# Gate tiles between the heads of the latent attention, and its values as hi/lo halves in f32r

## The reference, cut to what matters

```
proj = rmsnorm(x, ln_g) @ w_in
c_q, c_kv, k_rope, gate = split(proj, [384, 640, 672])
q  = rmsnorm(c_q) @ w_q_up
kv = rmsnorm(c_kv) @ w_kv_up            # k_nope and v per head
q, k = rope(rmsnorm(q)), rope(rmsnorm(concat(k_nope, k_rope)))
o  = causal_softmax_attention(q, k, v)
x  = x + (o * silu(gate)) @ w_out
```

## Time and profile before

| | us |
|---|---|
| median of 3 runs | 1353.39 (1350.48 to 1353.78) |
| the profiled execution, its own time | 1351.43 |
| its span from first to last instruction | 1349.6 |
| TensorE busy | 1317.7 (98%) |
| VectorE busy | 751.0 (56%) |
| ScalarE busy | 622.7 (46%) |
| GpSimd busy | 282.0 (21%) |

### The profile page before, as it was taken

How to read it: one execution, slowest core, us unless ns; L and a number is a source line. 1 busy time by engine, 2 the same in 40 slices (tenths; PEclk the granted TensorE clock), 3 DMA queues, 4 the chain that set the end, 5 groups by cost and what they waited for, 6 DMA issues and landing times. The chain is left out here.

```text
span 1349.6 us, 18281 instructions
## 1 busy us (share of the span) xinstructions
PE 1317.7 (98%) x6494; PEld 1095.5 (81%) x6494; DVE 751.0 (56%) x1236; ACT 622.7 (46%) x1108; POOL 282.0 (21%) x343
## 2 busy tenths in 40 slices
PE   7999999999999999999999999999999999999997
PEld 6989777788888888888888878888888888878876
DVE  5445688833753235798444643336467237578734
ACT  5336866622532234898244423424334224346534
POOL 2101844100000006674000000000000000677510
PEclk9999999999999999999999999999999999999999
DMA  5423200022222232001222323331333322311111
GB/s 189 115 67 106 70 1 0 1 94 94 94 94 94 94 98 88 18 0 32 103 101 93 95 78 98 105 94 51 95 108 103 110 94 63 110 43 37 35 60 63
DMA packets 63515, 104.05 MB, mean 77 GB/s; under 512 B 3428, under 2 KB 21080, under 8 KB 63320
## 3 DMA queue, kind: packets, MB, share of 16 engines
q1 hardware_dynamic: 62384, 99.44, 23.2%
q0 software_dynamic: 944, 3.65, 0.9%
q10 hardware_dynamic: 120, 0.05, 0.0%
HBM read 101.03 MB, written 2.10 MB: 76 GB/s over the span
## 5 line engine op out<-in xcount | busy, mean ns | idle before, releaser
L1531 DVE TENSOR_TENSOR w_lo<-stage,w_hi 128x1024 fp32r<-128x1024 f32 (+4 forms) x188 | 223.7, 1190 | 450.7 <-ACT w_hi L1016 450.7
L1016 ACT ACTIVATE w_hi<-stage 128x1024 fp32r<-128x1024 f32 (+4 forms) x188 | 191.8, 1020 | 475.4 <-PE ps L469 475.0
L467 PE MATMUL ps<-a0h,w_hi 128*128 128x512 f32 x448 | 177.4, 396 | 3.0 <-DVE q_lo L2061 3.0
L468 PE MATMUL ps<-a0l,w_hi 128*128 128x512 f32 x448 | 174.8, 390 | 0.0
L469 PE MATMUL ps<-a0h,w_lo 128*128 128x512 f32 x448 | 174.8, 390 | 0.0
L2133 POOL TENSOR_TENSOR small<-small 128x16 f32<-128x16 f32 (+2 forms) x15 | 33.4, 2224 | 504.2 <-DVE small L1609 360.0
L467 PEld LDWEIGHTS ps<-a0h,w_hi 128*128 128x128 f32 x448 | 84.4, 188 | 22.1 <-issue 4.7
L467 PE MATMUL ps<-w_hi,a0h 128*128 128x512 f32 x256 | 101.2, 395 | 0.0
L467 PE MATMUL ps<-a1h,w_hi 128*128 128x512 f32 x256 | 99.9, 390 | 0.3 <-DVE w_lo L1531 0.3
L469 PE MATMUL ps<-w_hi,a0l 128*128 128x512 f32 x256 | 99.7, 389 | 0.0
L468 PE MATMUL ps<-w_lo,a0h 128*128 128x512 f32 x256 | 99.6, 389 | 0.0
(11 more groups left out here) (313 smaller groups left out, 2980.4 us busy)
## 6 DMA issues: line engine op xcount, KB each, us to landing
stage<-in_a_w_in SPq DMA_DIRECT2D x48, 512.0 KB, 3.7
stage<-in_ple_w_gate SPq DMA_DIRECT2D x16, 512.0 KB, 3.3
stage<-in_w_kv_shared SPq DMA_DIRECT2D x16, 512.0 KB, 3.5
stage<-in_sb_w_in SPq DMA_DIRECT2D x16, 512.0 KB, 3.5
stage<-in_a_w_out SPq DMA_DIRECT2D x16, 512.0 KB, 3.3
stage<-in_b_w_in SPq DMA_DIRECT2D x16, 512.0 KB, 3.9
stage<-in_mla_w_in SPq DMA_DIRECT2D x8, 512.0 KB, 3.7
stage<-in_mla_w_out SPq DMA_DIRECT2D x8, 512.0 KB, 3.3
```

The lines of the kernel that those rows point to most:

```text
L467: pe.matmul(bank, wh, mh, start=start, stop=False)
L468: pe.matmul(bank, wh, ml, start=False, stop=False)
L1016: act.activation(slab(w_hi[r % 2], L, nk, w), slab(stage[r % 4], L, nk, w), ACT.Copy).then_inc(S("hi_ready"), 1)
L1531: dve.tensor_tensor(slab(w_lo[r % 2], L, nk, w), slab(stage[r % 4], L, nk, w), slab(w_hi[r % 2], L, nk, w), ALU.subtract)\
```

## The change

- `mla_gate` is cut in two. `mla_gate0` (tile 0) stands between `mla_cq` and `q_up`, `mla_gate1` (tiles 1 to 7) is made between the heads, two times two steps of k per head, in bank 7. The gate's loads are by tile: 128 columns of all eight row blocks.
- The transpositions of `proj` stand in `mla_cq` (8) and inside tile 0 (12). The squares are taken between the latents.
- The transposed probabilities are split: ScalarE rounds all 1280 columns to `prT_h`, VectorE subtracts to `prT_l`. The values of a head are 64 columns; `v_hl` holds their rounded half beside their rest as one operand of 128 columns (`mla_v` on ScalarE, `v_low` on GpSimd). A product therefore gives two halves of rows which have to be added: ScalarE copies one (`mla_part`), VectorE adds the other (`mla_sum`).
- Gate: VectorE scales a tile by half of the norm, ScalarE takes Tanh, GpSimd makes silu of it (`mla_silu`) and multiplies the head's output (`mla_gated`).
- One reciprocal for all four sums of a head; the scaled blocks follow after the last exponential.
- The transpositions of q and k go to bank 6, which the values use as well; q, k and values therefore wait for each other's readers.
- All steps of the heads are written out on every engine, without loops.
- The operand h of the layer stays in `a0h`, `a0l` (`H0 = A0`), and `pe_out0` moves.

The core of the diff:

```
@@ -192,12 +191,14 @@
     o_mh, o_ml = o_m[:, :, 0:T], o_m[:, :, T:2 * T]
     proj = put("proj", [P, MB, 672], 20)
     pr = put("pr", [P, TRI], 0)
-    prT = put("prT", [P, TRI], 5)
-    lat_sq = put("lat_sq", [P, MB, 672], 4)
+    prT_h, prT_l = put("prT_h", [P, TRI], 5, F32R), put("prT_l", [P, TRI], 4, F32R, of=SGM)
+    lat_sq = put("lat_sq", [P, MB, 672], 56)
     sq_tok = put("sq_tok", [P, MB, 4 * QK], 4, of=SGM)
     qT = [put(f"qT{s}", [P, T], 10 + 2 * s) for s in range(2)]
     kT = [put(f"kT{s}", [P, T], 14 + 2 * s) for s in range(2)]
-    v_pair = put("v_pair", [P, MB, P], 18)
+    q_tok_r = put("q_tok_r", [P, MB, HEADS * QK], 20, F32R)
+    v_hl = [put("v_hl0", [P, MB, P], 18, F32R), q_tok_r[:, :, 0:P]]
+    o_part = q_tok[:, :, 2 * QK:2 * QK + P]
     q_ring = [put(f"q_ring{s}", [P, MB, QK], 76 + 1.5 * s) for s in range(2)]
     k_ring = [put(f"k_ring{s}", [P, MB, QK], 79 + 1.5 * s) for s in range(2)]
     rope = put("rope", [P, 5, MB, ROPE], 82)
...
@@ -344,9 +345,10 @@
     LINEARS = [
         Linear("proj0", ins["ple_w_proj"][0], 2, columns(0, D), False, PT0, items("p0")),
         Linear("mla_cq", w_in, 8, columns(0, 672, 336), True, H0, items("h_mla")),
-        Linear("mla_gate", w_in, 8, columns(672, 1696), False, H0, items("h_mla")),
+        Linear("mla_gate0", w_in, 8, columns(672, 800), False, H0, items("h_mla"), by_tile=True),
         Linear("q_up", ins["mla_w_q_up"][0], 3, columns(0, HEADS * QK, 4 * QK), True, CQ[:3], IQ),
         Linear("kv_up", ins["mla_w_kv_up"][0], 2, columns(0, 2048), True, CQ[3:], IL),
+        Linear("mla_gate1", w_in, 8, [(800, 896)], False, H0, items("h_mla"), by_tile=True),
         Linear("out0", ins["mla_w_out"][0], 8, columns(0, D), False, OM, items("o_mla")),
         Linear("gate0", ins["ple_w_gate"][0], 8, columns(0, D), False, A1, items("x0")),
         Linear("sh_k", w_sh, 8, columns(0, D), False, A0, items("h_kv")),
...
+        def mla_gate_tile(L, j, bank, a, b):
+
+            r = L.load0 + j
+            if a == 0:
+                pe.wait_ge(S("lo_ready"), r + 1)
+                if j:
+                    pe.wait_ge(S("mla_gate1_read"), j)
+            wh, wl = slab(w_hi[r % 2], L, KD, P), slab(w_lo[r % 2], L, KD, P)
+            for k in range(a, b):
+                mm = three(ps[bank][:, :], wh[:, k, :], wl[:, k, :], *L.acts[k], k == 0, k == KD - 1)
+            if b == KD:
+                mm.then_inc(S("ring_used"), 1)
+
+        linear("mla_cq", 0, second={4: latents(0, 2)})
+        mla_gate_tile(lin["mla_gate0"], 0, 3, 0, 5)
+        latents(2, 5)()
+        mla_gate_tile(lin["mla_gate0"], 0, 3, 5, KD)
         linear("q_up")
...
+        def mla_values(h, first):
+            pe.wait_ge(S("pT_a"), 3 * h + 3)
+            pe.wait_ge(S("pT_b"), 3 * h + 3)
+            pe.wait_ge(S("v_ok"), h + 1)
+            pe.wait_ge(S("v_lo"), h + 1)
+            pe.wait_ge(S("kT_ok"), min(h + 3, HEADS))
             if not first:
                 pe.wait_ge(S("o_read"), h)
             for j in range(MB):
+                at = slice(KEY_COL[j], KEY_COL[j] + T - j * P)
+                pe.matmul(ps[6][:, j * P:T], v_hl[h % 2][:, j, :], prT_h[:, at], start=j == 0, stop=False, skip_group_check=True)
+                t = pe.matmul(ps[6][:, j * P:T], v_hl[h % 2][:, j, :], prT_l[:, at], start=False, stop=j == MB - 1, skip_group_check=True)
             t.then_inc(S("o_done"), 1)
 
+        def mla_step(h, s, i):
+
+            first, last = h == 0, h == HEADS - 1
+            mla_scores(h, s, first)
             if first:
                 pe.wait_ge(S(group_read[G + 3][0]), group_read[G + 3][1])
+            if not last:
+                mla_q(h + 1, 1 - s)
+            if i < PAIRS - 1:
+                mla_gate_tile(lin["mla_gate1"], i, 7, 4 * s, 4 * s + 2)
+            if not last:
+                mla_k(h + 1, 1 - s)
+            if i < PAIRS - 1:
+                mla_gate_tile(lin["mla_gate1"], i, 7, 4 * s + 2, 4 * s + 4)
             if not first:
+                mla_values(h - 1, h == 1)
+            mla_probs_T(h, first)
 
 
...
+        split_to(lin["q_up"].load0)
+        act.wait_ge(S("mla_cq_read"), 8)
+        latent_squares((0, 1))
+        latents(2, 4)
+        latent_squares((2, 3))
+        latents(4, 5)
+        split_to(lin["q_up"].load0 + 1)
+        act.wait_ge(S("mla_gate0_read"), 1)
+        act.activation(sgm[0][:, :], sgm[0][:, :], ACT.Silu).then_inc(S("sg_ready"), 1)
         act.wait_ge(S("lat_ok"), 1)
...
+            for b, (c, n) in enumerate(((0, T), (T, 384), (896, 384))):
+                act.activation(prT_h[:, c:c + n], ps[3 + b][:, 0:n], ACT.Copy).then_inc(S("pT_a"), 1)
...
+        def mla_step(h):
+            i, s = h // 2, h % 2
+            more = h < HEADS - 1
+            if h:
+                probs_T(h - 1)
+            probs(h, s, h == 0, (lambda: head_T(h + 1, 1 - s, "qT_done", qT, "q", "qT_ok")) if more else None)
+            if more:
+                head_T(h + 1, 1 - s, "kT_done", kT, "k", "kT_ok")
+            if h == 0:
                 k_squares(lin["kv_up"].n - 1)
-            if not first:
-                o_hi(i - 1, o_mh, "o_read", "o_mla")
-            probs(b, 1, between=None if last else lambda: head_T(a + 2, 0, "qT_done", qT, "q", "qT_ok"))
-            if not last:
-                head_T(a + 2, 0, "kT_done", kT, "k", "kT_ok")
-            probs_T(b)
-
-        mla_pair(0, first=True)
-        with act.Fori(1, PAIRS - 1) as i:
-            mla_pair(i)
-        mla_pair(PAIRS - 1, last=True)
+                mla_v(0)
+            if s == 0 and i < PAIRS - 1:
+                split_to(lin["mla_gate1"].load0 + i + 1)
+            if s == 0 and i:
+                mla_tanh(i)
+            if s and i:
+                o_hi(i - 1, o_mh, "o_gated", "o_mla")
+            if h:
+                mla_part(h - 1)
+            if more:
+                mla_v(h + 1)
...
+            dve.wait_ge(S("exp_done"), MB * h + MB)
+            link(dve.reciprocal(rsum, ssum))
+            for j in reversed(range(MB)):
                 at = slice(QRY_COL[j], QRY_COL[j] + (j + 1) * P)
                 dve.tensor_scalar(pr[:, at], pr[:, at], rsum[:, j:j + 1], None, ALU.mult).then_inc(S("p_ready"), 1)
...
-            dve.tensor_copy(prT[:, T:T + 384], ps[4][:, 0:384])
-            dve.tensor_copy(prT[:, T + 384:TRI], ps[5][:, 0:384]).then_inc(S("pT_b"), 1)
+            for b, (c, n) in enumerate(((0, T), (T, 384), (896, 384))):
+                dve.wait_ge(S("pT_a"), 3 * h + (b + 1))
+                dve.tensor_tensor(prT_l[:, c:c + n], ps[3 + b][:, 0:n], prT_h[:, c:c + n], ALU.subtract).then_inc(S("pT_b"), 1)
...
+        def mla_step(h):
+            i, s = h // 2, h % 2
+            maxima(h)
+            if h:
+                probs_T(h - 1)
+            normalize(h)
+            if h == 0:
                 head_sums(k_ss, 4 * HD, "k")(lin["kv_up"], G, MB - 1, None)
-            if not first:
+            if s == 0 and i < PAIRS - 1:
+                split_to(lin["mla_gate1"].load0 + i + 1)
+            if s and i < PAIRS - 1:
+                mla_gate_read(i + 1)
+            if s and i:
                 o_lo(i - 1, o_mh, o_ml, "o_mla")
-            normalize(b)
-            o_gate(a, 0, i, ps[6], "o_done", "o_read", "o_mla")
-            probs_T(b)
-
-        dve.wait_ge(S("sg_ready"), 8)
-        mla_pair(0, first=True)
-        with dve.Fori(1, PAIRS - 1) as i:
-            link.begin(i, 1, 16)
-            mla_pair(i)
-        link.end(PAIRS - 2)
-        mla_pair(PAIRS - 1)
+            if h:
+                mla_sum(h - 1)
...
+        for h in range(1, HEADS + 2):
+            if h > 1:
+                mla_gated(h - 2)
+            if h < HEADS:
+                v_low(h)
+            if h % 2 == 0 and 0 < h < HEADS:
+                mla_silu(h // 2)
+            if h + 3 < HEADS:
+                mla_head(h + 3, (h + 3) % 2, (h + 3) // 2)
+                pool.wait_ge(S("qk_ring"), 2 * h + 8)
 
...
```

More of the change, by code:

```diff
@@ L522, in group @@
                         pe.wait_ge(S("x_new"), 4 + n + 1)
+                    if L.name == "q_up" and g == k == 0 and n == 3:
+                        pe.wait_ge(S("mla_gate0_read"), 1)
                     mm = products(k, n)
@@ L698, in _ @@
         linear("kv_up", late={1: first_head})
-        mla_pair(0, first=True)
-        with pe.Fori(1, PAIRS - 1) as i:
-            mla_pair(i)
-        mla_pair(PAIRS - 1, last=True)
+        for h in range(HEADS):
+            mla_step(h, h % 2, h // 2)
         def on_the_way(l):
@@ L1152, in sin_cos, with latents, latent_squares @@
             act.activation(cos_t[:, :, :], turns, ACT.Sin).then_inc(S("sin_ok"), 1)
-        linear("mla_cq", extra=[nothing] * 3 + [the_masks, sin_cos])
-        def latent_squares():
-            act.wait_ge(S("mla_cq_read"), 8)
-            for m in range(MB):
+        def latents(a, b):
+            for s in items("latent", a, b):
+                hi(s)
```

(29 more changed lines are left out.)

167 lines of the change are left out of this document (81 added, 86 removed).

## The result

The changed kernel takes 1357.78 us (median of 10 runs, 1355.65 to 1361.47), the kernel before 1351.47 in the same series (10 runs, 1350.48 to 1353.78). The ratio is 1.0046, interval [1.0035, 1.0056]: slower by 6.3 us, more than the 0.3% that a measurement can tell. The ten executions of the changed kernel fall into two groups: four with a mean granted clock of 0.993 or 0.994 take 1355.7 to 1357.3 us, six with 0.989 take 1357.7 to 1361.5, and the profiled one is of the first group.

A forecast was written before the change was run, and what follows sets the result against it. TensorE was taken as the bound (13.77 of 14 us per pair), VectorE close behind. -38.15 + 0.9 + 35.2 - 0.9 = -3.0, plus 3.6 for waits on GpSimd, gave +0.6 on 1353.39: stated 1353.5 us, range 1343 to 1363.

The forecast's parts named there:

- rival 2: Head steps: VectorE's tail decides, 1.0 us lost per step instead of 0.3, so +8.4 us, 1362 us; chance 0.25.
- What leaves: Ahead of the attention: seven gate tiles leave, -38.15 us; a wait at the second q_up group adds 0.9.
- The values: Values of each head on TensorE: eight f32r matmuls take 1.25 us instead of eight fp32 passes of 2.16.
- Rival 3: Values on TensorE: f32r paced like fp32, 2.16 us, so 14 us are lost, 1368 us; chance 0.04.
- One step: One head on TensorE: 8.74 us of work, 9.1 with waits, equal to the first exponential's start + 6.36 us.
- The lock: VectorE's small products ahead of the exponentials wait for GpSimd's operation: 0.3 us per step over 12 steps, +3.6 us.
- the edges: First and last steps: step 0 7.6 us, step 1 11.2, step 14 9.05, step 15 7.1; values inside out0 -0.9.
- Tail: Ahead of out0: TensorE waits 2.95 us for copies, subtractions and a sum before the last low probabilities are ready.

The follow-up runs named there:

- the new form: Changed kernel with VectorE's scaled negatives taking the scale as a per-partition scalar, not as a second tensor operand: 1351.88 us, ratio 1.0005 to the kernel before.
- e11: Changed kernel with the new form, the fillers, the moved sums, and only ScalarE's qT copy moved behind the first exponential: 1347.25 us, ratio 0.9964 to the kernel before.
- The fillers: Changed kernel with unread matmuls filling TensorE's idle stretches in steps 14 and 15 and ahead of out0: 1353.66 us, ratio 1.0016 to the kernel before.
- The moved sums: Changed kernel with VectorE's sums of squares of the last k group moved from step 0 into step 1: 1356.37 us, ratio 1.0035 to the kernel before.
- The short GpSimd product: Changed kernel with GpSimd's gated output cut to 32 of 512 columns, old form of scaled negatives kept: 1354.60 us, ratio 1.0024 to the kernel before.

## Why the prediction was right or wrong

The forecast was 1353.5 us and no measurable change; it came out 1357.8 and slower, inside the range and on the side that had 0.29. By times alone the miss looks like 4.3 us. The forecast stood on 1353.39 us, the median of three executions; ten gave 1351.47. So the forecast change of +0.6 met one of +6.3, and 1.9 us of the miss were hidden by luck. Nor did it get slower by rival 2, the path that had the 0.25: the first exponentials of steps 2 to 13 start at +2.76 to +3.22, below the +3.3 that it asked for.

*What leaves.* Right: the first scores came 38.04 us earlier, forecast 38.15 - 0.9 = 37.25. The wait in q_up is there with 0.83 us (and one of 0.50 that I had not seen). The 0.8 us in favour are not a finding: the first scores start between 117.7 and 119.6 us in the runs whose code ahead of them is the same.

*The values.* Right: 1.24 us for 1.25, and fp32 values cost 12 us more. Rival 3 is out.

*One step.* Right as a formula, with a reason that bears less than I put on it. "Start of the first exponential + 6.36" holds to 0.05 us wherever kT's copy stays in its place: 9.49 - 3.13 and 9.11 - 2.76 in the changed kernel, 9.00 - 2.66 with the new form, 9.10 - 2.78 with qT's copy moved, and 10.00 - 2.73 = 7.27 with fp32 values, which is 6.36 + 0.9. The qT copy, on which I put the 0.40 us of loss, does hold the changed kernel (0.72 us in even steps, 0.34 in odd ones), but hardly more than kT's copy: without its wait the steps stayed. I had the values start as soon as kT's copy ends and gave them 0.2 us to spare. In e11, where they wait, they start 0.25 us after its end (187.45 against 187.20), in the changed kernel 0.36 in an odd step. The spare was 0.1 us.

*The lock.* Near in size, wrong in place: the exponentials are 0.37 us later in even steps and not at all in odd ones, 0.2 per step on average against my 0.3; with the form changed, 0.49 per even step came back. I had put GpSimd's short operations beside the product in odd steps and its long ones mostly past in even steps. It is the long one that stands there: the gated output starts at +1.76 of an even step (196.58 - 194.82) and at +5.17 of an odd one. Steps 2 to 13 took 111.8 us, forecast 112.8. That it also stretches the scaled blocks to about +8.3 in odd steps I had under rival 2; it is so (2.28 us for 1.28 in the changed kernel), and hidden until the blocks start later.

*The step that failed: the edges.* I summed them at full clock. "Step 14 has no gate tile but still waits for kT: 9.05" was 11.45; step 1 was 12.42 for 11.2; step 15 with the tail 11.27 for 10.05; and from out0 on, where I had -0.9, +0.9. Together 2.4 + 1.2 + 1.2 + 1.8 = 6.6 us, and 0.2 in step 0; steps 2 to 13 took 1.0 and the part ahead 0.8 less than forecast. That leaves 5.0, and the forecast +0.6 becomes the +5.7 of the traces. In step 1, in step 14 and ahead of out0 TensorE stood idle for 2 us or more and came back at 1.2 GHz. I had reckoned most of these waits myself; what I left out was to ask what they do to the clock where no gate piece stands in them. The fillers show this cause for 2.1 us in step 14, 0.3 in step 15 and 1.6 in out0, together their 4 us. The other 0.9 us of step 15 is not clock: it was still 10.94 with it at 1.00, so my chain for the tail was too short by that. For step 1 the half clock is read from the trace: its first exponential starts at +4.50, so that the formula gives 10.9 us, and the 1.6 above that is the clock. The moved sums took it away together with part of the wait.

*What the lock has to do with it.* Only in part shown. The new form saved 5.9 us. In its trace the even steps give 3.0 and steps 1 and 14, where the clock stayed up, about 4.5; step 15, where it fell, takes 1.1 back. The short GpSimd product saved the even steps too and, in its trace, not step 14. Whether the clock stays up at such waits differs between executions of one kernel, as the groups of the twelve show; no trace shows in which step the other executions kept it. A part of such differences has nothing to do with the change: one stretch of the second layer (from 1188 to 1202 us in the kernel before) takes 13.9 us there, 14.3 in the changed kernel's and 12.9 to 15.8 in the others, with unchanged code. So medians over many executions decide here, and single traces only say where.

*Tail.* Before out0 TensorE waits 2.81 us for copies and subtractions of the last probabilities, forecast 2.95: right. The excess of step 15 lies ahead of it.

## What to carry to other kernels

Work that fills the holes of one engine is worth least at the ends of its loop: look at the first and last passes, where the filling has run out, reckon the waits there, and ask what the clock does after them. When a small operation sits ahead of a chain that the whole stage waits for, its form matters more than its length: 0.2 us of work cost 3 to 6 us by its second tensor operand. And where a wait is removed, work out the next one to a tenth of a microsecond, and include the time from the end of a copy to the start of the work that waits for it, for here the next wait stood 2 us further on with the same sum.
